# One hybrid decoder layer: queries and keys projected as one pass over the weights, and the bias table's product moved among the first products

## The reference

```python
h = rmsnorm(x, pre_mix_norm[layer])
proj = h @ w_in[layer]                     # 1024 x 3072
rq, rk, rv, rg, mq, mk, mv = jnp.split(proj, split_at, axis=-1)
rq = rotary(rq...); rk = rotary(rk...) * (RET_QK_DIM ** -0.5)
ret = jax.nn.silu(rg) * head_rmsnorm(retention(rq, rk, rv))
moba = moba_attention(mq, mk, mv, rel_bias)     # 8 heads of 64, causal, bias from a table by distance
mix = jnp.concatenate([ret, moba], axis=-1) @ w_out[layer]
x = x + rmsnorm(mix, post_mix_norm[layer])
h = rmsnorm(x, pre_ffn_norm[layer])
f = (jax.nn.silu(h @ w_gate[layer]) * (h @ w_up[layer])) @ w_down[layer]
x = x + rmsnorm(f, post_ffn_norm[layer])
```

## Time and profile before

| what | us |
|---|---|
| median of three runs | 300.24 |
| profiled execution, its own time | 300.5 |
| its span, first to last instruction | 298.7 |
| outside the span in that execution | 1.8 |
| PE busy | 292.1 (98% of the span) |
| DVE busy | 188.7 (63%) |
| ACT busy | 153.5 (51%) |
| POOL busy | 12.0 (4%) |
| transfers | 63.07 MB, 211 GB/s over the span |

### The profile page before, as it was taken

One profiled execution on the slowest core, in us unless ns is written; L12 is line 12 of the kernel. 1 busy time (PEld: TensorE's weight loads), 2 busy tenths in 40 slices (PEclk: granted clock), 3 DMA queues, 4 the chain that ended last, 5 costly groups with the idle time before them and its releaser, 6 DMA issues.

```text
span 298.7 us, 4149 instructions
## 1 busy us (share of the span) xinstructions
PE 292.1 (98%) x1420; PEld 236.6 (79%) x1420; DVE 188.7 (63%) x283; ACT 153.5 (51%) x245; POOL 12.0 (4%) x20
## 2 busy tenths in 40 slices
PE   8999999999999999999999999999999999999992
PEld 3788877787888888888888888888888888888881
DVE  3867467796879679878492936557383737451246
ACT  5989567647464645595280815254362626330331
POOL 0030000000020013200000000000000000000001
PEclk9999999999999999999999999999999999999998
DMA  6999995208635460659888694958667594415003
GB/s 203 397 408 385 407 379 175 108 2 284 216 135 174 176 214 0 215 182 343 322 272 273 209 306 168 262 195 232 237 216 233 189 295 157 127 47 164 0 2 140
DMA packets 24026, 63.07 MB, mean 211 GB/s; under 512 B 2724, under 2 KB 7885, under 8 KB 24013
## 3 DMA queue, kind: packets, MB, share of 16 engines
q1 hardware_dynamic: 23616, 61.78, 60.8%
q0 software_dynamic: 304, 1.06, 1.0%
q10 hardware_dynamic: 92, 0.05, 0.1%
HBM read 59.46 MB, written 3.42 MB: 211 GB/s over the span
## 4 chain that ended last, share of the span: by engine, by line
PE 97%; DVE 1%; DVEq 0%; ACT 0%; issue 0%
PE bank L1024 29%; PE bank L1026 28%; PE bank L1025 28%; PE bank L1072 2%; PE bank L1056 1%; PE bank L1076 1%; PE bank L1080 1%; PE bank L1034 1%; PE bank L1043 1%; PE bank L1139 1%; PE bank L1184 1%; DVE res L1015 1%; DVE res L1009 1%; PE bank L1169 1%; PE bank L1193 0%; PE bank L1194 0%
## 5 line engine op out<-in xcount | busy, mean ns | idle before, releaser
L1024 PE MATMUL bank<-w_hi,a_hi 128*128 128x512 f32 x256 | 101.0, 394 | 0.0
L1026 PE MATMUL bank<-w_hi,a_lo 128*128 128x512 f32 x256 | 99.9, 390 | 0.0
L1025 PE MATMUL bank<-w_lo,a_hi 128*128 128x512 f32 x256 | 99.6, 389 | 0.0
L1024 PEld LDWEIGHTS bank<-w_hi,a_hi 128*128 128x128 f32 x256 | 48.1, 188 | 10.4 <-issue 0.7
L1026 PEld LDWEIGHTS bank<-w_hi,a_lo 128*128 128x128 f32 x256 | 48.1, 188 | 10.3
L1025 PEld LDWEIGHTS bank<-w_lo,a_hi 128*128 128x128 f32 x256 | 48.1, 188 | 9.8
L918 DVE TENSOR_TENSOR w_lo<-raw,w_hi 128x1024 fp32r<-128x1024 f32 x40 | 47.8, 1235 | 0.9 <-ACT w_hi L633 0.9
L724 DVE TENSOR_TENSOR w_lo<-raw,w_hi 128x1024 fp32r<-128x1024 f32 x32 | 37.8, 1221 | 12.8 <-ACT w_hi L492 12.8
L633 ACT ACTIVATE w_hi<-raw 128x1024 fp32r<-128x1024 f32 x40 | 40.3, 1052 | 2.7 <-DMA raw<-in_w_gu 2.7
L1024 PE MATMUL bank<-d_hi,h_hi 128*128 128x512 f32 x88 | 34.4, 391 | 0.0
L1025 PE MATMUL bank<-d_lo,h_hi 128*128 128x512 f32 x88 | 34.4, 390 | 0.0
(11 more groups left out here) (111 smaller groups left out, 261.8 us busy)
## 6 DMA issues: line engine op xcount, KB each, us to landing
raw<-in_w_gu SPq DMA_DIRECT2D x44, 512.0 KB, 5.2
raw<-in_w_dn SPq DMA_DIRECT2D x22, 512.0 KB, 5.4
raw<-in_w_in SPq DMA_DIRECT2D x20, 512.0 KB, 8.2
raw<-in_w_out SPq DMA_DIRECT2D x8, 512.0 KB, 3.8
h_rows<-hid_sq SPq DMA_DIRECT2D x9, 256.0 KB, 2.0
hid_T<-h_rows SPq DMA_DIRECT2D x36, 64.0 KB, 4.1
raw<-in_w_in SPq DMA_DIRECT2D x8, 256.0 KB, 5.2
xs<-in_x SPq DMA_DIRECT2D x2, 512.0 KB, 8.1
```

Of the source, the lines that this page charges most:

```text
L1024: pe.matmul(acc, hi, wh, start=first, stop=False)
L1025: pe.matmul(acc, hi, wl, start=False, stop=False)
L1026: return pe.matmul(acc, lo, wh, start=False, stop=last)
```

## The change

- **Joint units.** Queries and keys take units 0 to 7 together. A unit is now one block of 128 rows, its first half the 512 columns of the queries, its second half those of the keys. Each x block is used for 12 matmuls rather than 6. Queries accumulate in `pj[0]`, keys in `pj[1]`, both are complete with unit 7. The bytes and the number of matmuls stay the same.
- **x in smaller steps.** SP loads x block n with unit n for n = 0 to 3, then two blocks each ahead of units 4 and 6. ACT and DVE split blocks 0 to 3 before their loop and blocks 4 to 7 at steps u=0 to 3.
- **The bias product** stands behind 8 warm-up products of 512 columns and is followed by 4 of 128 columns (`FILL`); before there were 10 of 512 and the bias product came after block k=0. ACT issues the load of the table (`rel`) before that of the constant (`bucket`); it was the other way round.
- **The norm of x later.** `xs` is loaded ahead of units 8 and 9, `ident` ahead of unit 9; squares and factors are at steps u=5 and 6 (`SQ_U`), `nq` at u=7. ACT writes out queries and keys together at u=8.
- **Banks.** Values accumulate in `po` rather than `pj[0]`, so group 2 waits for no copy; keys are turned into `pj[0]` rather than `po`; the wait for the values' copy moves from after unit 14 to after unit 13.

The core of the diff:

```diff
...
 RING = 8
 DRING = 4
 HALVED = 4
-WARM = 10
+JOINT = 2
+XS_N, SQ_U = 8, 5
+WARM, FILL = 8, 4
 LEAD = 4
 LO_UNITS = {15: [], 16: [], 17: [], 18: [19, 20], 19: [21, 22], 20: [23, 24]}
...
+        def projected(group):
+            return po if group == JOINT else pj[group % 2]
...
         def wait_projection(eng, group, t):
-            if t == 0:
+            if t == 0 or group == 0:
                 eng.wait_ge(proj_done, group + 1)
...
-                if 5 <= n < 5 + NT:
-                    sp.dma_start(xs[:, n - 5, :], x[(n - 5) * P:(n - 4) * P, :]).then_inc(x_loaded[n - 5], 16)
...
+                if XS_N <= n < XS_N + NT:
+                    t = n - XS_N
+                    sp.dma_start(xs[:, t, :], x[t * P:(t + 1) * P, :]).then_inc(x_loaded[t], 16)
+                if n == XS_N + 1:
                     sp.dma_start(ident[:, :], ident_c).then_inc(ident_loaded, 16)
...
                     for i in range(KPU):
                         sp.dma_start(raw[:, n, i * CW:(i + 1) * CW], w_in[n][:, i * CW:(i + 1) * CW]
                                      ).then_inc(raw_half[n] if i == 0 else raw_loaded[n], 16)
-                        if n == 0:
-                            load_x(i, i + 1, xt_first if i == 0 else xt_loaded[0])
-                        elif i == 0:
-                            load_x(KPU * n, KPU * (n + 1), xt_loaded[n])
-                elif n < NK // KPU:
-                    load_x(KPU * n, KPU * (n + 1), xt_loaded[n])
-                    load(n, n % RAW, w_in[n])
+                        if i == 0:
+                            load_x(n, n + 1, xt_loaded[n])
                 else:
+                    if n < NK and n % KPU == 0:
+                        load_x(n, n + KPU, xt_loaded[n])
                     load(n, n % RAW, w_in[n])
...
+            act.dma_start(rel[0:BUCKETS, :], rel_bias).then_inc(rel_loaded, 16)
             act.dma_start(bucket[:, :], bucket_c).then_inc(rel_loaded, 16)
-            act.dma_start(rel[0:BUCKETS, :], rel_bias).then_inc(rel_loaded, 16)
...
+            def x_high(k):
+                wait_x_block(act, k)
+                act.activation(a_hi[:, k, :], x_block(k), ACT.Copy, scale=gain(k)).then_inc(x_hi, 1)
+
+            for n in range(LEAD):
+                if n < HALVED:
+                    act.wait_ge(raw_half[n], 16)
+                    act.activation(w_hi[:, n, 0:CW], raw[:, n, 0:CW], ACT.Copy).then_inc(hi_half, 1)
+                    x_high(n)
+                    wait_raw(act, n)
+                    act.activation(w_hi[:, n, CW:UNIT], raw[:, n, CW:UNIT], ACT.Copy).then_inc(hi_ready, 1)
+                else:
+                    x_high(n)
+                    hi_in(n)
...
-                    act.activation(dst[:, t, :], pj[group % 2][:, t, :], ACT.Copy,
+                    act.activation(dst[:, t, :], projected(group)[:, t, :], ACT.Copy,
...
-                    act.activation(by_half(kT, 0), from_half(po, 0), ACT.Copy).then_inc(kT_ready, 1)
+                    act.activation(by_half(kT, 0), from_half(pj[0], 0), ACT.Copy).then_inc(kT_ready, 1)
...
-                if u == UPG:
+                if u == JOINT * UPG:
...
                     rows_out(qn, 0, lambda t: nq[:, t:t + 1], q_nat)
-                if u == 2 * UPG:
                     rows_out(kn, 1, r_x, k_nat)
...
+                if u + LEAD < NK:
+                    x_high(u + LEAD)
                 for n in HI_UNITS.get(u, [u + LEAD]):
                     hi_in(n)
                 if u == 0:
                     act.wait_ge(brow_done, 1)
                     act.activation(brow[:, :], wk[0:MH, 0, 0:REV], ACT.Copy).then_inc(brow_ready, 1)
-                if u < NT:
-                    act.wait_ge(w_used, 1)
-                    act.wait_ge(x_loaded[u], 16)
+                if SQ_U <= u < SQ_U + NT:
+                    t = u - SQ_U
+                    act.wait_ge(x_loaded[t], 16)
                     for c in range(2):
-                        squares(X_, u, c, xs[:, u, c * CW:(c + 1) * CW])
+                        squares(X_, t, c, xs[:, t, c * CW:(c + 1) * CW])
...
+            for n in range(LEAD):
+                if n < HALVED:
+                    half_low(n, slice(0, CW), hi_half, lo_half)
+                    x_low(n)
+                    half_low(n, slice(CW, UNIT), hi_ready, lo_ready)
+                else:
+                    x_low(n)
+                    lo_in(n)
...
+                if u + LEAD < NK:
+                    x_low(u + LEAD)
                 if u <= RS_U:
                     for n in LO_UNITS.get(u, [u + LEAD]):
                         lo_in(n)
-                if u < NT:
-                    factor(X_, u, 2 * u + 2)
-                if u == NT:
+                if SQ_U <= u < SQ_U + NT:
+                    factor(X_, u - SQ_U, 2 * (u - SQ_U) + 2)
+                if u == SQ_U + NT:
                     wait_factor(dve, X_, NT - 1)
...
+            bias_row_product()
+            for _ in range(FILL):
+                pe.matmul(bank67[:, 0, 0:P], ones[:, 0:P], ones[:, 0:P], start=True, stop=True)
+
             def first_unit(u):
 
-                for i in range(KPU):
-                    k, cols = KPU * u + i, slice(i * CW, (i + 1) * CW)
+                for i in range(JOINT):
+                    acc, cols = pj[i], slice(i * CW, (i + 1) * CW)
                     pe.wait_ge(hi_half if i == 0 else hi_ready, u + 1)
-                    pe.wait_ge(x_hi, k + 1)
+                    pe.wait_ge(x_hi, u + 1)
                     for t in range(NT):
-                        pe.matmul(pj[0][:, t, :], a_hi[:, k, tile(t)], w_hi[:, u, cols],
-                                  start=(k == 0), stop=False)
+                        pe.matmul(acc[:, t, :], a_hi[:, u, tile(t)], w_hi[:, u, cols],
+                                  start=(u == 0), stop=False)
                     pe.wait_ge(lo_half if i == 0 else lo_ready, u + 1)
                     for t in range(NT):
-                        pe.matmul(pj[0][:, t, :], a_hi[:, k, tile(t)], w_lo[:, u, cols],
+                        pe.matmul(acc[:, t, :], a_hi[:, u, tile(t)], w_lo[:, u, cols],
                                   start=False, stop=False)
-                    pe.wait_ge(x_lo, k + 1)
+                    pe.wait_ge(x_lo, u + 1)
                     for t in range(NT):
-                        ins = pe.matmul(pj[0][:, t, :], a_lo[:, k, tile(t)], w_hi[:, u, cols],
-                                        start=False, stop=(k == NK - 1))
-                        if t == 0 and k == NK - 1:
+                        ins = pe.matmul(acc[:, t, :], a_lo[:, u, tile(t)], w_hi[:, u, cols],
+                                        start=False, stop=False)
+                ins.then_inc(w_used, 1)
+
+            def joint_unit(u):
+
+                pe.wait_ge(lo_ready, u + 1)
+                pe.wait_ge(x_lo, u + 1)
+                last = u == NK - 1
+                for i in range(JOINT):
+                    for t in range(NT):
+                        ins = product(pj[i][:, t, :], a_hi[:, u, tile(t)], a_lo[:, u, tile(t)],
+                                      w_hi[:, u % RING, i * CW:(i + 1) * CW],
+                                      w_lo[:, u % RING, i * CW:(i + 1) * CW], first=False, last=last)
+                        if last and (i, t) in ((0, 1), (1, 0)):
                             ins.then_inc(proj_done, 1)
-                    if k == 0:
-                        bias_row_product()
                 ins.then_inc(w_used, 1)
 
-            for u in range(N_IN):
-                g, s = divmod(u, UPG)
-                if u < HALVED:
-                    first_unit(u)
-                else:
-                    pe.wait_ge(lo_ready, u + 1)
-                for t in range(0 if u < HALVED else NT):
+            def projection_unit(u, g, s):
+
+                pe.wait_ge(lo_ready, u + 1)
+                for t in range(NT):
                     if s == 0:
 
-                        if g == 2:
-                            pe.wait_ge(q_nat, t + 1)
                         if g == 3:
                             pe.wait_ge(l_ready, 2)
                         if g == 4:
@@ -1104,16 +1125,21 @@
                             pe.wait_ge(rT_ready, NT)
                     for i in range(KPU):
                         k = KPU * s + i
-                        if g == 0 and t == 0:
-                            pe.wait_ge(x_lo, k + 1)
-                        ins = product(pj[g % 2][:, t, :], a_hi[:, k, tile(t)], a_lo[:, k, tile(t)],
+                        ins = product(projected(g)[:, t, :], a_hi[:, k, tile(t)], a_lo[:, k, tile(t)],
                                       w_hi[:, u % RING, i * CW:(i + 1) * CW],
                                       w_lo[:, u % RING, i * CW:(i + 1) * CW],
                                       first=(k == 0), last=(k == NK - 1))
...
+            for u in range(N_IN):
+                if u < HALVED:
+                    first_unit(u)
+                elif u < NK:
+                    joint_unit(u)
```

(9 more changed lines are left out.)

53 lines of the change are left out of this document (16 added, 37 removed).

## The result

| | before | changed |
|---|---|---|
| median of 20 runs, us | 300.24 | 301.18 |
| lowest to highest | 299.93 to 300.86 | 299.79 to 301.9 |
| profiled execution, its own time | 300.5 | 301.05 |
| its span | 298.7 | 299.3 |

The ratio of changed to before is 1.0022, 95% interval 1.0014 to 1.0029. In the medians it is 0.94 us, and 301.18 lies above the range of 299.1 to 300.8. The spread tells as much as the median: the runs of before lie within 0.93 us, those of the changed kernel within 2.11, 13 of 20 above 301.0. The profiled execution is one of the 13.

A forecast was written before the change was run, and what follows sets the result against it. PE's stream was taken as the bound: 0.93 us gained from the bias product, less the longer front's cost, with 0 for joint units and norm. Taking a gain of 0.64, 300.24 - 0.64 = 299.6 us, range 299.1 to 300.8.

The forecast's parts named there:

- What bounds the kernel now: Whole kernel: PE's stream, busy 98% of the span; only the first 9.65 us had something to gain.
- The bias product's 0.93 us: Behind block k=0: taking the bias product out of PE's stream gains 0.93 us.
- the second half of unit 0 asks for less than before: Unit 0 at the start: x's block 1 no longer needed, so nothing else there would be late.
- The front: PE's start: front ends about 5.94, first real matmul at 6.05, costing up to 0.76 us; net gain 0.57.
- with the change of pace at 6.4 again: PE's start: clock rises at 6.4 us as before, so unit 0's twelve matmuls end at 9.08, against 9.65.
- rival (b): PE's start: clock rises later, after idling or small products; slower by 1.4, 301.6 us; chance 0.09.
- Does the constant arrive?: Load of bucket ahead of the bias product: lands by 4.47 at the latest, PE idles 0 to 0.26 us, taken as 0.
- The norm moved: 0, but it is what is late next: Units 8 to 14: no stall; keys ready at 33.5 with slack 0.7 us, bias load by 39.7 at worst.
- rival (a): Turn of the keys: PE waits if the squares and nq chain is over 0.7 us later; chance 0.11.
- Joint units: 0.: Units 0 to 7: same matmuls, bytes and pace, so 0 us.
- weights come earlier against PE: First four joint units: transfers carry 640 KB per unit rather than 768 KB.
- Range: Whole kernel: 299.1 to 300.8 us, leaving out (b), the worst of (a) and a tail of a shorter front.

The follow-up runs named there:

- h3: Kernel before with the bias product made from high and low parts of the table, two products behind block k=4; 300.82 us, ratio 1.0016.
- e4: Changed kernel with the bias load ahead of the two factors on GpSimd's queue; 301.36 us, ratio 1.0023.
- e1: Kernel before with the changed kernel's front alone, table loaded before the constant; 300.48 us, ratio 1.0014.
- e3: Changed kernel with the norm of x back where it was, loads ahead of units 5 and 6, squares at steps 0 and 1; 300.00 us, ratio 1.0003.
- g4: Joint units alone: changed kernel with the front and the norm's place of the kernel before; 300.16 us, ratio 0.9994.
- k1: e2 with the bias load ahead of the two factors on GpSimd's queue; 300.40 us, ratio 1.0005.
- g2: e3 with the bias table padded by zeros from 8 to 128 columns, so the product fills all output rows; 300.39 us, ratio 1.0010.
- e2: Changed kernel with the front of the kernel before, norm still late; 301.23 us, ratio 1.0032.
- g3: Kernel before with 8 warm-up products rather than 10 and nothing in their place; 301.93 us, ratio 1.0054.
- g1: Kernel before with a front of 11 products of 512 columns and 4 of 128, bias product where it was; 300.46 us, ratio 1.0001.
- h2: g1 with three front products replaced by one full-size plain float32 product of 384 columns; 300.44 us, ratio 0.9998.
- h1: g1 with three of its 512-column front products made thin, bf16 with 33 rows and 8 output rows; 301.44 us, ratio 1.0028.
- i2: e3 with the bias product padded to 128 rows and 128 output rows; 302.30 us, ratio 1.0082.
- i4: i2 with 9 products of 512 columns ahead of the bias product and 1 of 128 behind, rather than 8 and 4; 301.40 us, ratio 1.0034.
- i1: e3 with the bias product's operands padded from 33 to 128 rows, still 8 output rows; 302.22 us, ratio 1.0063.

## Why the prediction was wrong, point by point

- **"What bounds the kernel now"** held for before. The bias product's 0.93 us was measured right as a stretch of PE's time, and in before's trace it was all cost; in other runs part of it covers a wait for x's block 1, 0.79 us in h3. For the joint kernel my step that the second half of unit 0 asks for less than before was right: PE did not wait for it. That unit 1 started 1.02 us earlier in the profiled execution and not 0.57 is luck of that run: the pace had changed by 4.83.
- **The front: the first step that failed.** The length was right: in e4 the product took 1.38 us at the low pace (I took 1.30) and the first real matmul came at 6.04 (predicted 6.05). What failed is the step "with the change of pace at 6.4 again". I held the rise fixed while I changed what PE does ahead of it. Across runs the gain of up to 1 us and the loss of some 1.4 us in the late ones cancel: e1 1.0014 (0.9999 to 1.0028, so the forecast gain of 0.0019 is excluded), and e3 over g4 0.0009. This was rival (b), with its mechanism; I gave it 0.09, for a gap, and wrote that the product's place among real matmuls, after the rise, spoke against it. That row could say nothing of the time ahead of the rise. The Trainium skill ("TensorE: Matmul & The Clock Gate", section "What's actually happening") says that the number of matmuls before the rise differs between runs of one kernel; by this the trace of before, one execution, was no basis for a fixed 6.4. No kernel here has two traces, but those that run the same products up to the rise agree: with the front of before it came at about 3.5 us in k1 and 6.4 in before, with the new front by 3.94 in e1 and at about 8.9 in e4.
- **"Does the constant arrive?"** I set 4.47 as the latest, from a transfer of five times the bytes. It landed at 4.83, 3.6 us after its issue at 1.20, and left a gap of 0.47 us. More bytes are no upper bound for fewer: the half unit was issued first of all. In the other traces with this front it was there in time, by 3.94 in e1 and by 4.29 in e3, e4 and g2, so the gap belongs to some runs only. The landing at 3.3 us that I worked out from the Trainium skill ("DMA: Bandwidth & Descriptors", section "Anatomy of one DMA — SWDGE (gpsimd) path") was farther off than 4.47 in the changed kernel's trace; the measurement decides.
- **"The norm moved: 0, but it is what is late next": the second step that failed.** The right chain and the wrong sizes. Unit 9's weights were usable at 25.24, not 23.4. The running sum reached their 7.46 MB at some 23.0 us rather than 22.2 (323 GB/s over the first 22.9 us), and the lag behind it, 1.1 us by the one landing that I had, was 2.2 here; why it doubled is not shown. Keys were ready at 34.7, not 33.5. The bias load took 10.6 us as allowed, but from 30.83: 41.4, not 39.7. I then asked only for the first waiter (two heads' logits for group 3, at 42.0) and not for the next: from the first logits to the last normalised head ACT and DVE take 7.84 us in both kernels (39.40 to 47.24, 41.45 to 49.29), and the turn behind unit 13 lost 0.33 us. By e2, k1 and g4, with the front of before, this branch is some 0.8 of the 1.1 us of the norm's price. The keys' copy, on which rival (a) rested, shows where PE comes early, as in the profiled execution; how the price divides with the new front is open (e4).
- **Joint units: 0.** Right as a part alone in the middle of the runs (g4 0.9994), but "weights come earlier against PE" was argued from bytes and not followed to the low parts. Unit 4's was done at 17.15 (16.40 in before) and 0.39 us late for the early PE, and g4's trace waits for those of units 5 and 6.
- **Range.** Both failing terms have one sign, and I added them to no case together. By the ratios the front came to between +0.4 us (e1) and -0.3 (the changed kernel against e2), with +0.3 between (e3 against g4), where I had a gain of 0.57; the norm costs 0.6 us with the new front (the changed kernel against e3) and 1.1 with that of before (e2 against g4), where I had 0. Each of these is uncertain by some 0.5 us. Taken in order, joint units -0.2, front +0.3, norm +0.6, they give the 0.7 us of the ratio 1.0022.

## What to carry to other kernels

A step moved off the critical chain takes along everything queued behind it on its engine: here two tiny factors moved by ten microseconds on GpSimd and held a 1 MB load on the same queue. Ask for its last consumer, not its first, and put a load that needs nothing of the moved step ahead of it. In this kernel the front that warms TensorE did best when it was dense, of full-size products and without a gap ahead of the rise; judge one by 10 or more runs, since a change that moves the rise of the clock shows as two groups and not in one profile. Before taking work out of a stretch, look for what arrives within it.

## What the runs showed of the hardware that was not expected

- The low level of TensorE's clock (0.43 us for 512 columns) lasted until between 3.5 (k1) and 12.3 us (g3) in the traces, always with a first product at 0.78 or 0.79. With full-size products and at most 0.3 us of gap ahead of the rise (before, g1, g4, k1, h2) nearly all runs lie within about 1.2 us; with a thin product of 1.4 us there (e1, e3, g2, h1) a third to a half are 1.2 to 2 us slower; with a gap of 0.66 us (g3) the runs spread over 4.3 us. That the slower runs are those with a late rise is shown by the traces of e4, g2, h1, g3, i2 and i4 (upper group, low pace to 8.9 us or beyond) and of e1, e3 and i1 (lower group, risen by 5.6); for the other runs it is inferred. Behind the rise idle time did no such harm: PE stood 1.0 us in e1 and k1 and 1.5 in i1 and went on at the high pace.
- The granted clock by slice reads full speed in these stretches, so only the distances between starts show the level.
- A plain float32 product of 384 columns stands in the trace as two records of 0.37 us at the high level (before) and 0.69 at the low (e4); the same as two float32r products takes 0.44 us in all (h3).
- A transfer of 50 KB issued at 1.2 us beside the weights' stream landed 3.6 us later in the changed kernel's trace, longer than the first 256 KB took (3.0 there, 3.35 in before), but within 2.7 us in e1's.
